# Triangular inverses on 32x32 diagonal blocks, and four ada products between their steps

## The reference

```python
# rwkv7_mixer: six heads of 64 channels, one state S (64x64) each, a scan over 256 tokens
def step(S, inp):
    r_t, d_t, k_t, v_t, kk_t, a_t = inp
    sa = jnp.einsum('bhij,bhj->bhi', S, -kk_t)
    S = S * d_t[:, :, None, :] + sa[..., None] * (kk_t * a_t)[:, :, None, :] + v_t[..., None] * k_t[:, :, None, :]
    return S, jnp.einsum('bhij,bhj->bhi', S, r_t)
# s5_mixer: a complex state-space recurrence of 16 groups over the same tokens
_, _, s_re, s_im = lax.associative_scan(_complex_linear_combine, (a_re, a_im, bu_re, bu_im), axis=1)
# second_block, needed much later: modulation vectors from the condition c
mod = cond @ ada_w[layer] + ada_b[layer]
kv_shift, kv_scale = jnp.split(cond @ kv_ada_w + kv_ada_b, 2, axis=-1)
```

## Time and profile before

| | us |
|---|---|
| median of 3 runs (1309.79 to 1317.23) | 1310.95 |
| the profiled execution, its own time | 1307.66 |
| span of the profiled execution | 1305.9 |
| busy: TensorE matmuls / weight loads | 1254.2 / 1119.7 |
| busy: VectorE / ScalarE / GpSimd | 601.3 / 653.2 / 846.8 |

### The profile page before, as it was taken

The page is one execution under the profiler, slowest core; times in us unless marked ns, Lnnn a source line. Parts: engine busy times, 40 slices in busy tenths (PEclk is TensorE's granted clock), DMA queues, the critical chain, the costliest instruction groups (busy, mean ns, idle before and its releaser), DMA issues.

```text
span 1305.9 us, 24860 instructions
## 1 busy us (share of the span) xinstructions
PE 1254.2 (96%) x10093; PEld 1119.7 (86%) x10093; DVE 601.3 (46%) x1369; ACT 653.2 (50%) x1074; POOL 846.8 (65%) x445
## 2 busy tenths in 40 slices
PE   6997988889999999999999999999999999999998
PEld 6993547679899999999988889998988789988887
DVE  6658687642676695432555512412111114555411
ACT  5531343125755554654666643656554554655642
POOL 8984500025788877664788777667765655888782
PEclk8998999989999999999999999999999999999999
DMA  8859895603465555435555566443648893455550
GB/s 263 214 169 376 316 343 209 212 29 102 158 194 177 171 178 186 162 129 162 161 191 183 175 194 194 130 147 113 194 134 262 266 294 120 160 189 193 178 177 33
DMA packets 232943, 242.76 MB, mean 186 GB/s; under 512 B 9196, under 2 KB 201854, under 8 KB 232830
## 3 DMA queue, kind: packets, MB, share of 16 engines
q1 hardware_dynamic: 232510, 241.08, 57.0%
q10 hardware_dynamic: 320, 0.10, 0.0%
HBM read 240.11 MB, written 1.05 MB: 185 GB/s over the span
## 4 chain that ended last, share of the span: by engine, by line
PE 80%; DVE 5%; ACT 2%; issue 1%; POOL 1%; DMA 0%; DVEq 0%; SPq 0%; ACTq 0%
PE banks L572 79%; DVE arena L1804 1%; DVE banks L1804 1%; DVE arena L1797 1%; PE banks L1428 1%; ACT ring_hi L2569 1%; POOL ring_lo L1716 1%; ACT arena L2569 1%; DVE hn_lo L1804 1%; DMA ring<-in_w_kv_dram 0%; DVE banks L1797 0%; DVE arena L1810 0%; PE banks L582 0%; PE banks L914 0%; PE banks L1037 0%
## 5 line engine op out<-in xcount | busy, mean ns | idle before, releaser
L1716 POOL TENSOR_TENSOR ring_lo<-ring,ring_hi 128x2048 fp32r<-128x2048 f32 (+1 forms) x176 | 717.1, 4090 | 393.4 <-ACT ring_hi L2569 392.9
L2569 ACT ACTIVATE ring_hi<-ring 128x2048 fp32r<-128x2048 f32 (+1 forms) x176 | 300.1, 1706 | 113.0 <-PE banks L572 70.2
L572 PE MATMUL banks<-hn_hi,ring_lo 128*128 128x256 f32 x1160 | 321.1, 284 | 0.0
L572 PE MATMUL banks<-hn_hi,ring_hi 128*128 128x256 f32 x992 | 279.7, 288 | 7.0 <-ACT hn_hi L2569 3.1
L2569 ACT ACTIVATE arena<-banks 128x256 f32<-128x256 f32 (+6 forms) x350 | 134.2, 399 | 275.9 <-PE banks L572 212.8
L572 PE MATMUL banks<-hn_lo,ring_hi 128*128 128x256 f32 x992 | 257.5, 284 | 0.0
L572 PEld LDWEIGHTS banks<-hn_hi,ring_lo 128*128 128x128 f32 x1160 | 221.9, 192 | 0.1
L572 PEld LDWEIGHTS banks<-hn_hi,ring_hi 128*128 128x128 f32 x992 | 191.5, 193 | 10.7 <-issue 4.4
L572 PE MATMUL banks<-hn_pair,ring_hi 128*128 128x512 f32 (+1 forms) x768 | 183.4, 374 | 0.1
L572 PEld LDWEIGHTS banks<-hn_lo,ring_hi 128*128 128x128 f32 x992 | 180.5, 193 | 0.1
L572 PEld LDWEIGHTS banks<-arena 64*32 64x32 f32 (+6 forms) x1698 | 108.8, 155 | 63.8 <-issue 39.5
(11 more groups left out here) (286 smaller groups left out, 1909.5 us busy)
## 6 DMA issues: line engine op xcount, KB each, us to landing
ring<-in_ada_w_dram SPq DMA_DIRECT2D x48, 1024.0 KB, 9.1
ring<-in_ffn_w_up_dram SPq DMA_DIRECT2D x44, 1024.0 KB, 5.2
ring<-in_w_up_dram SPq DMA_DIRECT2D x22, 1024.0 KB, 5.2
ring<-in_w_kv_dram SPq DMA_DIRECT2D x34, 512.0 KB, 4.3
ring<-in_ffn_w_down_dram SPq DMA_DIRECT2D x16, 1024.0 KB, 5.3
ring<-in_w_in_dram SPq DMA_DIRECT2D x9, 1024.0 KB, 8.2
ring<-in_attn_w_q_dram SPq DMA_DIRECT2D x18, 512.0 KB, 4.0
ring<-in_kv_ada_w_dram SPq DMA_DIRECT2D x8, 1024.0 KB, 7.0
```

The lines of the kernel that those rows point to most:

```text
L572: return nc.tensor.matmul(o, l, r, start=start, stop=stop, **k)
L1716: led.emit(g.tensor_tensor(low, raw, high.bitcast(F32), ALU.subtract), sem("lo_ready"))
L2569: led.emit(nc.scalar.activation(o, x, func, **k), signal, value)
```

## The change

The inverse keeps only what is not zero. The matrices lie as `CHUNKS`, each 128 partitions (chunk r, row) x 2 (p) x 6 (s, c) x 32. `chunk_grams` computes only the diagonal 32x32 blocks of N and L, and each step of `inverse_step` is one group in one bank: 48 matmuls of 32x32x32, each on the diagonal tile (32r, 32r) of the array. One copy, on VectorE or on ScalarE, takes a whole step. The two transposes become products with a 32x32 identity, `chunk_ident`, which GpSimd copies together at the start with the masks' diagonal blocks. `solved` splits each of its matmuls in four in the same way. Four ada products leave the state-space rounds 1, 3, 5 and 7 and stand between the inverse's steps, behind N2, Y1, Ya and Yb.

```diff
@@ state-space rounds (TensorE)
-                ada()
+                if j % 2 == 0:
+                    ada()
@@ grams and steps (TensorE)
+            def chunk_grams():
+                halves = [(opened(("NL", p)), slice(64 * p, 64 * p + 64)) for p in range(2)]
+                for x, (lw, rw) in enumerate(((7, 6), (6, 7))):
+                    for s in range(2):
+                        for c in range(3):
+                            o = 192 * x + 32 * (3 * s + c)
+                            for r in range(4):
+                                cut = slice(s * P + 32 * r, s * P + 32 * r + 32)
+                                for p, (b, q) in enumerate(halves):
+                                    last = mm(b[32 * r:32 * r + 32, o:o + 32], W[lw][q, c, cut], W[rw][q, c, cut],
+                                              tile_position=(64 * p, 32 * r))
+                close(last, 2)
             def inverse_step(name, lw, rw):
-                for s in range(2):
-                    for p in range(2):
-                        b = opened((name, s, p))
-                        for c in range(3):
-                            o = b[:, c * P:c * P + P]
-                            if rw is None:
-                                last = nc.tensor.transpose(o, tmat(s, lw)[:, p, c, :], ident[:, :])
-                            else:
-                                last = mm(o, tmat(s, lw)[:, p, c, :], tmat(s, rw)[:, p, c, :])
-                        close(last)
+                b = opened(("inv", name))
+                for p in range(2):
+                    for m in range(6):
+                        o = 192 * p + 32 * m
+                        for r in range(4):
+                            q = slice(32 * r, 32 * r + 32)
+                            right = chunk_ident[q, :] if rw is None else CHUNKS[rw][q, p, m, :]
+                            last = mm(b[q, o:o + 32], CHUNKS[lw][q, p, m, :], right, tile_position=(32 * r, 32 * r))
+                close(last)
@@ solved
-                        last = mm(b[:, c * P:c * P + P], KEEP[s][3][:, p, c, :], AM[s][:, c, :, p * HD:p * HD + HD])
+                        for r in range(4):
+                            q = slice(32 * r, 32 * r + 32)
+                            last = mm(b[q, c * P:c * P + P], CHUNKS[9][q, p, 3 * s + c, :],
+                                      AM[s][q, c, :, p * HD:p * HD + HD], tile_position=(32 * r, 32 * r))
@@ order of the steps
-                elif name in ("T8", "T16"):
+                if name in ('N2', 'Y1', 'T8', 'Ya', 'T16', 'Yb'):
                     ada()
@@ constants (GpSimd, ahead of the tables)
+            for r in range(4):
+                q = slice(32 * r, 32 * r + 32)
+                led.settle()
+                led.emit(g.tensor_copy(chunk_ident[q, :], ident[q, q]))
+            for r in range(1, 4):
+                q = slice(32 * r, 32 * r + 32)
+                led.settle()
+                led.emit(g.tensor_copy(masks[q, 0:4, 0:32], masks[q, 0:4, q]))
@@ copies of a step (VectorE; ScalarE takes L2, L4, T8t, T16t)
-                for s in range(2):
-                    for p in range(1 if add is None else 2):
-                        b = take((name, s, p))
...
+                if name not in ON_SCALAR:
+                    b = shaped(take(("inv", name))[:, 0:384], 12, 32)
+                    if add is None:
+                        copy(both(CHUNKS[to]), b, *freed(("inv", name)))
+                    else:
+                        tt(both(CHUNKS[to]), b, both(CHUNKS[add]), ADD, *freed(("inv", name)))
```

More of the change, by code:

```diff
@@ L208, in two_block_kernel @@
         W = [at(M0 + 768 * i, 3, T) for i in range(12)]
[L209 to L213, removed]
+        CHUNKS = [at(M0 + 384 * i, 2, 6, 32) for i in range(9)] + [at(M0 + 14592, 2, 6, 32)]
+        KEEP = [[at(M0 + 12288 + 768 * i, 2, 3, P) for i in range(3)],
+                [at(M0 + 3072, 2, 3, P), at(M0 + 3840, 2, 3, P), place("hn_a", HN, F32, 2, 3, P)]]
         tok4 = [at(M0 + 9216, 4, 3, P), at(5664, 4, 3, P)]
@@ L483, in two_block_kernel @@
                      "Ya": ("T8",), "T16": ("T8t", "Ya"), "T16t": ("T16",), "Yb": ("T16",), "T32": ("T16t", "Yb")}
-        def tmat(s, i):
-            return KEEP[s][3] if i == 9 else TM[s][i]
+        ON_SCALAR = ("L2", "L4", "T8t", "T16t")
         @block.tensor
@@ L1121, in _ @@
             pe.wait_ge(sem("gram_in"), 1)
-            for s in range(2):
-                gram("N", s)
-                gram("L", s)
+            chunk_grams()
             pe.wait_ge(sem("tri_first"), 4)
-            for s in range(2):
-                for p in range(2):
-                    copied(("N", s, p))
             for name, lw, rw, _add, _dst in INV:
@@ L2188, in three, with each, both @@
                 return shaped(b[:, 0:384], 3, P)
[L2190 to L2196, removed]
+            def each(m, n):
+                return m[:, 0:32].unsqueeze(1).broadcast_to([P, n, 32])
+            def both(x):
+                return x.rearrange("p a b c -> p (a b) c")
+            for p in range(2):
+                b = take(("NL", p))
+                tt(CHUNKS[0][:, p], shaped(b[:, 0:192], 6, 32), each(U8, 6), MUL, sem("tri_first"))
+                tt(CHUNKS[1][:, p], shaped(b[:, 192:384], 6, 32), each(L8M, 6), MUL, sem("tri_first"))
             settle()
-            for s in range(2):
-                for p in range(2):
-                    tt(TM[s][7][:, p], TM[s][0][:, p], over3(ident[:, :]), ADD, sem("tri_ready") if p else None)
+            tt(both(CHUNKS[7]), both(CHUNKS[0]), each(chunk_ident, 12), ADD, sem("tri_ready"))
             def masked(names, s):
@@ L2208, in _ @@
             for name, _l, _r, add, to in INV:
[L2209 to L2215 removed]
+                if name not in ON_SCALAR:
[4 more added lines that the diff above has]
+                        tt(both(CHUNKS[to]), b, both(CHUNKS[add]), ADD, *freed(("inv", name)))
                 if name == "N2":
[L2217 to L2220, removed]
+                    for p in range(2):
+                        dve.wait_ge(*freed(("NL", p)))
+                    tt(both(CHUNKS[2]), both(CHUNKS[3]), each(L16M, 12), MUL)
                     settle()
[L2222 to L2224 removed]
+                    tt(both(CHUNKS[3]), both(CHUNKS[3]), each(L32M, 12), MUL, sem("tri_low"))
             masked((("MT", 0, U32S), ("Rb", 1, U32I), ("Rk", 2, U32I)), 0)
@@ L2595, in reach @@
                     if n < 2:
[L2596 to L2597 removed]
+                        act_.wait_ge(*freed(("inv", "T32")))
                     for x in before:
@@ L2815, in _ @@
             for name, _l, _r, add, dst_ in INV:
-                if add is None:
-                    for s in range(2):
-                        b = take((name, s, 1))
-                        af(tmat(s, dst_)[:, 1], shaped(b[:, 0:384], 3, P), ACT.Identity, *freed((name, s, 1)))
+                if name in ON_SCALAR:
+                    b = take(("inv", name))
+                    af(CHUNKS[dst_].rearrange("p a b c -> p (a b c)"), b[:, 0:384], ACT.Identity, *freed(("inv", name)))
                 if name in ("Y1", "Ya"):
```

26 lines of the change are left out of this document (13 added, 13 removed).

## The result

The changed kernel takes 1331.28 us (median of 4 runs, 1330.19 to 1334.67), the kernel before in the same runs 1312.67 us (1309.79 to 1317.23). The ratio is 1.0145, 95% interval [1.011, 1.018]: 19 us slower, where 13 us faster were forecast. The profiled execution took 1330.19 us, with a span of 1328.5 us and a mean granted clock of 0.965. The trace before is of an execution of 1307.66 us, 5 us under the median beside it, so some of the 22.6 us between the two spans is scatter.

The account below looks back on a forecast made before the run. TensorE was taken to bound the kernel, with four fifths of the span on it. The inverse's 12.5 us plus 0.4 us from the two other edits made 12.9, so 1310.95 - 12.9 = 1298 us, range 1290 to 1310.

Parts of the forecast that it names:

- the cost of the inverse: First grams to the ada product at 245.94, 40.98 us before: 14.4 us less by compute, 12.5 after load waits.
- so I cost the waits at nothing: Inverse steps: products or transposes cover the 0.56 us copy before each dependent step; without cover, about 0.9 us each.
- The start rate: Rival in inverse steps and grams: small tiles cost 15 ns and not 8, 9 us, total 1305; chance 0.10.
- Four tiles don't overlap: Rival in every inverse step: diagonal tiles run singly, 28 ns a record, 14 us slower, total 1325; chance 0.08.
- the 25 ns between starts: Skill's rule on matmul starts: a step would cost 2.4 us, the grams 4.8, total 1317, 6 us slower.
- the one bank: Skill's rule for inverse steps: row tiles can't use one PSUM bank at the same time; no size of its own.
- The loads: In the inverse, products behind Yb and Rk wait for their second chunks, taking back 1.9 us of the gain.
- The rounds: State-space rounds: without two late products, the transpose of scores at 146.84 comes at about 145.5, gaining 1.3 us.
- The clock rival: Rounds, 139 to 155: half the clock reaches there, 3 to 7 us of gain gone, total 1303; chance 0.09.
- a sign of being wrong: Steps of over 2 us, or a low granted clock between 139 and 155, would prove the forecast wrong.
- The seven copies: GpSimd, ahead of the sine and cosine tables: tables move from 89.90 to about 91.0, delaying VectorE's rounds 0.9 us.
- Everything behind: Everything behind the H and E products: some 13 us earlier, otherwise the same.

Follow-up runs that it names:

- light loads: The changed kernel, with 7/8 of the bytes left out of the ada products' loads from the 15th on: 1314.16 us, ratio 1.0033.
- products-only kernel: The kernel before with only the four ada products moved, its inverse unchanged: 1321.22 us, ratio 1.0073.
- inverse-only kernel: The changed kernel with its ada products put back where the kernel before has them, the 32x32 inverse kept: 1320.85 us, ratio 1.0091.
- 64x64 blocks: The changed kernel with 64x64 diagonal blocks, products at their old places, three GpSimd copies placed late: 1298.73 us, ratio 0.9883; repeated, 1301.07 us, 0.9914.

## Why the prediction was wrong

**The step that failed is the cost of the inverse: "8 ns, by the row nearest in shape: 0.8 us a step", with "so I cost the waits at nothing".** It has no term for the supply of instructions. The rate itself was nearly right: steps start 0.95 us apart when fed (234.98 to 235.93), the grams took 1.82 us for an expected 1.8, and the first step began at 3.07 us for 3.0. The error was to take a rate read from a burst of 32 records as what TensorE holds over 2500 instructions. The prediction asked which engine, transfer or tile would be late, and not who brings the instructions.

By its sum the product behind Rk starts 26.6 us behind the first gram, and 28.5 with 1.9 us of waiting for loads; it starts at 59.2 (268.15 - 208.94), and no product waits for a load. Of the 32.6 us between 26.6 and 59.2, gaps are 20.8. Products, transposes and the first MT gram at half the clock are 7.3 (products 3.64, 3.29, 2.25 and 3.33 for 1.92; 2 x 0.67; 1.1), the steps at 0.95 for 0.8 another 1.7. Of the 2.8 left, an estimate of 1.4 goes to small tiles at half the clock (15 to 17 ns a record in the rows from 215.88, 219.61 and 241.43, for 10); the rest is unexplained.

**The rivals.** "The start rate" is not what was measured: 15 ns a record is seen at half the clock alone, 10 at the full one, and its 9 us cover no gap. "Four tiles don't overlap" is refuted: 96 records in 0.95 us, 10 ns each, although all four tiles of a step write one bank. So neither the 25 ns between starts nor the one bank costs anything to be seen here. The slower outcome came from a mechanism that was not on the list.

**The loads.** The 1.9 us were not paid; the stage was too slow to need them. The loads did harm where the prediction did not look: half of the gaps (light loads: 10.4 for 20.8 us).

**The rounds.** A gain of 1.3 us became none in the products-only kernel, and with the copies a loss of 4.0. In the products-only trace the transpose that was at 146.84 is at 146.25, half of the gain; in the kernel after it is at 149.55.

The clock rival came true in its place, 139 to 155, which the prediction called a sign of being wrong. After and before:

```profile
139.00:155.00 16.00, 16.00 (x94) 7.63 (x97) 11.09 (x33) 6.45 (x20) 8.96 (x48) 0.79 0.57 186
```

```profile
139.00:155.00 16.00, 16.00 (x116) 7.64 (x108) 10.73 (x31) 8.28 (x24) 11.06 (x55) 1.00 1.01 368
```

TensorE is busy throughout, so 0.79 for 1.00 costs at most 3.4 us of 16. All seven kernels without the products of rounds 1, 3, 5 and 7 have 0.79 to 0.89 there, the four with them 0.97 to 1.00; and from 115 to 129 the same seven have 0.51 to 0.63 and the four 0.79 to 0.88. So less work on TensorE in the rounds goes with a lower clock, which is enough to take the gain (in the products-only kernel, at 0.89, up to 1.8 us). It does not explain all of the 2.7 us by which the transpose comes late: VectorE starts on the tables 1.35 us late, and the inverse-only kernel, with its products in the rounds, has the transpose at 149.58 too.

The rest of the 4.0 us is lost behind 172, at 0.91 and 0.77 of the clock in the windows from 172 and from 190 for 1.00 and 0.89 before. That can't be laid on the change: the second profile of the 64x64 blocks, whose products are in the rounds, has the same 0.91 and 0.77, the first 1.00 and 0.89.

**The seven copies**, 0.9 us forecast: VectorE starts 1.35 us later than before, of which moving them gave back 0.5. The direction was right, but not all of it is theirs: the tables are ready at 91.43 after, at 90.79 with the copies moved, and at 89.90 before. What makes the other 0.9 us is open.

**Everything behind** shifts by the same 22.7 us, as forecast in kind: TensorE bounds the rest.

Still open: what sets the half clock behind 172, why some packets come 3.5 us apart and some 5 with the same light loads, why one comes 3.65 us behind the last beside full loads, and what a product in place of the gap at 217.17 does.

## What to carry to other kernels

Count instructions, not only work. Cutting the matmuls into small tiles left TensorE less work but doubled or quadrupled what it must be fed in each step; here it was fed 256 instructions (128 fp32 records with their weight loads) in 3.4 to 4.2 us where the DMA engines were nearly idle, mostly in 5.5 to 7.6 us beside full loads. A stretch that asks for more stalls in gaps with no releaser, 256 instructions or a multiple apart. The page shows them as idle time ended by "issue" and as more packets of the instruction queue. Of the three cuts tried, 128, 64 and 32, the best is the one whose instruction rate nearly fits, tiles of 64, and not the smallest.

## What the runs showed of the hardware

- Instruction packets of 16 KB on q8, in the stage of the kernel after at the soonest 3.4 us after one another (DMA share 0.09), three in a row 6.0 to 6.4 us beside the ring's loads (share 1.01 to 1.04), but once 3.65 us beside them; a starved TensorE goes on 2.3 to 2.6 us after such a packet begins.
- Where TensorE starves it is also granted less clock: 0.77 over the stage after, 1.00 over the same stage of the kernel before and 0.96 to 1.00 in the three with 64x64 blocks. At half the clock a product costs up to 3.6 us for 1.9. That adds some 7 us to the 21 of the gaps.
- Four 32x32 tiles on the array's diagonal run at once with one bank for all: 10 ns a record; two 64x64 tiles 32 ns (1.55 us for 48), where a full 128x128 record took 111.
